# Encoder trunk on one core: in each attention step the 18 gate products stand directly behind the scores

## The chip, the core and the metric

The kernel runs on one core of a Trainium2 chip. A core has TensorE (PE, matrix products and transposes), VectorE (DVE), ScalarE (ACT), GpSimd (POOL) and SyncE (SP), each with its own list of instructions that it works through in the order written; they meet only at semaphores. Products land in PSUM, which has eight banks. The metric is the device time of one execution in microseconds (us); lower is better.

## What is computed

Two layers work on 256 tokens of width 1024. Each layer first mixes tokens in three branches (latent attention with 8 heads, a spatial gating branch, attention to a memory of 256 rows with 4 heads), weighs each branch by a sigmoid gate per channel, and adds the result; then comes a feed-forward part, dense in the first layer and with 8 experts in the second.

```python
def memory_branch(q_raw, mem_n, w_mkv):
    q = q_raw.reshape(b, s, X_HEADS, X_HEAD_DIM) * (X_HEAD_DIM ** -0.5)
    kv = mem_n @ w_mkv
    sc = jnp.einsum('bshd,bmhd->bhsm', q, k).astype(jnp.float32)
    pr = jax.nn.softmax(sc, axis=-1).astype(v.dtype)
    return jnp.einsum('bhsm,bmhd->bshd', pr, v).reshape(b, s, BRANCH_WIDTH)

for l in range(DEPTH):
    h = rmsnorm(x, g_mix[l])
    p = h @ w_in[l]
    c_q, c_kv, k_r, z_sg, q_x, gate_logits = jnp.split(p, SPLITS, axis=-1)
    y_a = mla_branch(c_q, c_kv, k_r, positions, ...)       # 8 heads
    y_b = spatial_gating_branch(z_sg, g_sg[l], w_s[l], b_s[l])
    y_c = memory_branch(q_x, mem_n, w_mkv[l])              # 4 heads
    ys = jnp.stack([y_a, y_b, y_c], axis=2)
    yd = jnp.einsum('bsnw,nwd->bsnd', ys, w_br[l])
    gates = jax.nn.sigmoid(gate_logits.reshape(b, s, N_BRANCH, d) + b_gate[l])
    x = x + jnp.sum(gates * yd, axis=2) @ w_out[l]
    ...
```

## The kernel before

All products are float32 made of three: each operand is split into a high part (`whi`, made by ACT in `hi_parts`) and the rest (`wlo`, made by DVE in `lo_parts`), and high by high, high by rest and rest by high are summed. Weights come in pieces of 1 MB. There are three pairs of `whi`/`wlo` buffers, so a piece can be split when the piece three before it has been used up on PE.

The change is in the attention part of the mixer, which each of the two layers passes once (about 104 to 200 us and 532 to 628 us in the trace). There the heads' work is interleaved with the products of the gates and of the branch outputs. `mixer_steps` writes the order, and PE, ACT and DVE all walk through this one list:

- The memory heads: step i holds `ms` i (scores of head i), `mpT` i-1 (transposes of the softmax of the head before), `mo` i-2 (its product with the values, of the head before that) and one `fill`.
- The transposes `qT` and `kT` of queries and keys.
- The latent heads: step i holds `as` i (scores), `apT` i-1, `O` i-2 and one `fill`.

A `fill` is 18 products of `branch`, which the text below calls the 18 gate products though some are of a branch output. Four fills (parts 0 to 3) make one half of one branch: 48 gate products (tokens t=0 and t=1 in banks 6 and 7), then 24 output products (`br`, 12 for t=0 and 12 for t=1). The gate sum for t=0 ends with part 1, that for t=1 in part 2. The `br` sum for t=1 starts with the seventh product of part 3, and takes a PSUM bank there. The 16 fills stand in the 6 steps of the memory part and the 10 of the latent part. Products 0 to 15 in the texts are fills 0 to 15.

What ACT and DVE do for each entry of the list:

- `ms`/`as`: DVE takes the row maximum from the bank (`rmax`, then `nmax`), ACT the exponential (`pbuf`, line 1558). For memory heads DVE also multiplies by the reciprocal sum (line 2031), and `mpT` waits for that.
- `mpT`/`apT`: ACT copies the transposed softmax out of its bank (line 1566), which frees the bank and is what `mo`/`O` reads. This is called copy i below.
- `mo`: ACT writes `yT_hi` (line 1575), DVE `yT_lo` (line 2042). DVE then also rotates queries (lines 1975 to 1980) behind `mo` 0 and 1, and keys behind `mo` 2.
- `fill` of part 1 or 2: DVE adds the gate bias (`gate_add`, line 1987), then ACT takes the tanh (`gate_tanh`, line 1537). Part 3: DVE multiplies gate and output (`gate_merge`, line 1998).
- Before an entry, ACT and DVE split those weight pieces whose buffer is free by then (`room`).

PSUM banks are given out by `plan_psum`, which walks through the same list: scores, transposes, `mo` and `br` take the low bank that was given out longest ago. So the order of the list sets the banks too. `claim` on PE waits until the bank's last reader has freed it.

Of the kernel before, what the change touches and what calls it, by code (L numbers as in the profile page):

```python
# [60 lines left out]
def plan_psum(depth, heads, x_heads, fcd, nblk):  # L61
# [16 lines left out]
    for l in range(depth):  # L78
# [24 lines left out]
        for step in mixer_steps(heads, x_heads):  # L103
            if step[0] == "fill":
                n, half, part = filled(step[1])
                if part == 0:
                    for t in range(2):
                        take(("gate", l, n, half, t), bank=6 + t)
                elif part > 1:
                    take(("br", l, n, half, part - 2), oldest=low, held=4)  # L110
            elif step[0] in ("as", "apT"):
                take((step[0], l) + step[1:], oldest=low)
            elif step[0] != "O":
                take((step[0], l) + step[1:], oldest=(0, 1, 2, 3, 4, 5))
# [80 lines left out]
def mixer_steps(heads, x_heads):  # L195


    steps = []
    fill = list(range(16))
    for i in range(x_heads + 2):  # L200
        if i < x_heads:
            steps.append(("ms", i))
        if i == 0:
            steps += [("k", 0), ("k", 1), ("v", 0), ("v", 1)]
        if 1 <= i <= x_heads:
            steps.append(("mpT", i - 1))
        if i >= 2:
            steps.append(("mo", i - 2))
        steps.append(("fill", fill.pop(0)))
    for n in range(2):  # L210
        for t in range(2):
            steps += [("qT", t, n), ("kT", t, n)]
    for i in range(heads + 2):
        if i < heads:
            steps.append(("as", i))
        if 1 <= i <= heads:
            steps.append(("apT", i - 1))
        if i >= 2:
            steps.append(("O", i - 2))
        steps.append(("fill", fill.pop(0)))  # L220
    assert not fill
    return steps


def build(nc, x, mem, positions, g_mix, w_in, g_q, g_kv, w_uq, w_uk, w_uv, g_sg, w_s, b_s, g_mem,
# [21 lines left out]
    JOBS = NE * (-(-SEQ // CAP))  # L247
    QS, XS = QK ** -0.5, (BW // XH) ** -0.5
    steps = mixer_steps(H, XH)
    groups = plan_psum(DEPTH, H, XH, FCD, NM)  # L250

# [2109 lines left out]
```

## Time and profile before

| | |
|---|---|
| median of 3 runs | 1666.54 us (1666.48 to 1667.35) |
| the profiled execution's own time | 1666.63 us |
| its span, first to last instruction | 1664.5 us |
| PE busy | 1645.5 us, 99% of the span |
| DVE busy | 1286.9 us, 77% |
| ACT busy | 1057.5 us, 64% |
| longest waits of PE in the attention part | 0.57 and 1.72 us, in each layer |
| granted TensorE clock, mean | 0.998 |

PE is busy nearly all the time. Where it is idle within the attention part, the trace names what it waited for. A row of the timeline gives the start, the duration, engine and line, and in brackets the idle time before it and what ended that. The trace gives an instruction's own duration, but successors on ACT and DVE often start about 0.1 us before it ends; so the distance from start to start is used where two rows follow each other directly.

### The profile page before, as it was taken

Reading aid. Unit: us, or ns where it says so; the run is one execution under the profiler, and the core shown is the slowest. Engines: PE = TensorE matmul, PEld = TensorE weight load, DVE = VectorE, ACT = ScalarE, POOL = GpSimd, SP = SyncE. Lnnn points to the kernel's source line nnn. Section 1 sums busy time; section 2 is a strip of 40 time slices with the busy share of each in tenths; the row PEclk is TensorE's granted clock in tenths of the full one; section 3 lists DMA queues with packets and bytes.
Section 4 is the critical chain, followed back from the end, with each engine's and each line's share of the span. In section 5 each row is a group of like instructions: output and inputs, shape, how many; then the busy total and the mean of one; then the engine's idle time right before and its main releaser. Section 6 shows DMA issues by size and latency. Waiting matters only on the chain.

```text
span 1664.5 us, 22805 instructions
## 1 busy us (share of the span) xinstructions
PE 1645.5 (99%) x8464; PEld 1398.3 (84%) x8464; DVE 1286.9 (77%) x1163; ACT 1057.5 (64%) x961; POOL 30.0 (2%) x57
## 2 busy tenths in 40 slices
PE   9999999999999999999999999999999999999997
PEld 8988889999899788888888888888888888888885
DVE  7576567555566747698888888888888888888997
ACT  6554436433465454477777777777777777777775
POOL 1000000000000000020000000000000000000100
PEclk9999999999999999999999999999999999999999
DMA  7753488885366435699999999999999999999994
GB/s 234 230 169 136 140 279 299 270 263 191 103 198 194 144 128 176 253 357 393 395 394 390 354 395 388 359 391 385 364 380 385 372 394 360 387 380 366 396 393 160
DMA packets 243426, 496.98 MB, mean 299 GB/s; under 512 B 8534, under 2 KB 64400, under 8 KB 243360
## 3 DMA queue, kind: packets, MB, share of 16 engines
q1 hardware_dynamic: 237360, 479.23, 80.2%
q0 software_dynamic: 2624, 8.45, 1.6%
q10 hardware_dynamic: 3376, 8.39, 1.3%
q8 instruction: 44, 0.72, 0.2%
q14 instruction: 22, 0.18, 0.0%
HBM read 476.64 MB, written 19.40 MB: 298 GB/s over the span
## 4 chain that ended last, share of the span: by engine, by line
PE 91%; DVE 4%; ACT 2%; issue 2%; DMA 1%; DVEq 0%; POOL 0%; ACTq 0%
PE bank L1142 25%; PE bank L681 20%; PE bank L1175 19%; PE bank L1146 12%; PE bank L852 9%; PE bank L1159 1%; DVE wlo L1804 1%; PE bank L671 1%; ACT whi L1423 1%; PE bank L966 1%; DMA hn<-in_mem 1%; ACT pbuf L1558 0%; PE bank L938 0%; PE bank L1187 0%; DVE rmax L2023 0%
## 5 line engine op out<-in xcount | busy, mean ns | idle before, releaser
L2218 DVE TENSOR_TENSOR wlo<-raw,whi 128x2048 fp32r<-128x2048 f32 x328 | 748.1, 2289 | 108.0 <-ACT whi L1660 108.0
L1660 ACT ACTIVATE whi<-raw 128x2048 fp32r<-128x2048 f32 x328 | 627.7, 1918 | 177.4 <-PE bank L1146 94.1
L1804 DVE TENSOR_TENSOR wlo<-raw,whi 128x2048 fp32r<-128x2048 f32 (+3 forms) x121 | 259.4, 2148 | 183.5 <-ACT whi L1423 182.2
L1142 PE MATMUL bank<-whi,yT_hi 128*128 128x512 f32 x896 | 352.5, 396 | 0.0
L1142 PE MATMUL bank<-whi,yT_lo 128*128 128x512 f32 x896 | 347.4, 390 | 0.0
L1423 ACT ACTIVATE whi<-raw 128x2048 fp32r<-128x2048 f32 (+3 forms) x121 | 217.7, 1803 | 134.6 <-PE bank L681 100.4
L1146 PE MATMUL bank<-wlo,yT_hi 128*128 128x512 f32 x896 | 240.0, 390 | 0.0
L1146 PEld LDWEIGHTS bank<-wlo,yT_hi 128*128 128x128 f32 x896 | 168.2, 188 | 35.6
L1142 PEld LDWEIGHTS bank<-whi,yT_lo 128*128 128x128 f32 x896 | 168.3, 188 | 33.7 <-DVE yT_lo L2186 0.2
L1142 PEld LDWEIGHTS bank<-whi,yT_hi 128*128 128x128 f32 x896 | 168.3, 188 | 33.5
L1175 PE MATMUL bank<-whi,yT_hi 128*128 128x512 f32 x448 | 176.0, 393 | 0.0
L1175 PE MATMUL bank<-wlo,yT_hi 128*128 128x512 f32 x448 | 174.6, 390 | 0.0
L1175 PE MATMUL bank<-whi,yT_lo 128*128 128x512 f32 x448 | 174.5, 390 | 0.0
L681 PE MATMUL bank<-hT_hi,whi 128*128 128x256 f32 x464 | 131.4, 283 | 0.0
L681 PE MATMUL bank<-hT_hi,wlo 128*128 128x256 f32 x464 | 131.3, 283 | 0.0
L681 PE MATMUL bank<-hT_lo,whi 128*128 128x256 f32 x464 | 131.3, 283 | 0.0
L1175 PEld LDWEIGHTS bank<-whi,yT_hi 128*128 128x128 f32 x448 | 84.0, 188 | 25.2 <-issue 8.7
L1175 PEld LDWEIGHTS bank<-wlo,yT_hi 128*128 128x128 f32 x448 | 84.1, 188 | 17.8
L1175 PEld LDWEIGHTS bank<-whi,yT_lo 128*128 128x128 f32 x448 | 84.1, 188 | 16.2
L681 PEld LDWEIGHTS bank<-hT_lo,whi 128*128 128x128 f32 x464 | 89.0, 192 | 0.4
L681 PEld LDWEIGHTS bank<-hT_hi,whi 128*128 128x128 f32 x464 | 89.0, 192 | 0.4
L681 PEld LDWEIGHTS bank<-hT_hi,wlo 128*128 128x128 f32 x464 | 89.0, 192 | 0.0
(287 smaller groups left out, 2016.7 us busy)
## 6 DMA issues: line engine op xcount, KB each, us to landing
raw<-in_moe_w SPq DMA_DIRECT2D x336, 1024.0 KB, 7.4
raw<-in_w_in SPq DMA_DIRECT2D x36, 1024.0 KB, 5.1
raw<-in_dense_w SPq DMA_DIRECT2D x30, 1024.0 KB, 6.6
raw<-in_w_br SPq DMA_DIRECT2D x12, 1024.0 KB, 5.1
raw<-in_w_out SPq DMA_DIRECT2D x8, 1024.0 KB, 5.1
rows_by_slot<-qxT SPq DMA_DIRECT2D x15, 512.0 KB, 7.1
raw<-in_w_mkv SPq DMA_DIRECT2D x6, 1024.0 KB, 8.4
y_by_slot<-qxT SPq DMA_DIRECT2D x9, 512.0 KB, 7.7
```

What stands on the lines that cost most here:

```text
L671: ins = nc.tensor.matmul(bank, lhs(k), rhs(k), start=(k == 0), stop=(k == n - 1))
L681: ins = nc.tensor.matmul(bank, lhs(a, k), rhs(b, k), start=(start and k == chunks[0] and a + b == 0), stop=(stop and k == chunks[-1] and a ...
L852: ins = nc.tensor.matmul(bank, src(a, x0), w[b_][:, w0, :], start=(start and q + i == 0), stop=(stop and last))
L966: ins = nc.tensor.matmul(b[:, t * SEQ:(t + 1) * SEQ], qT[0:QK, h, tok(t)], kT[0:QK, h, :], start=True, stop=True)
L1142: nc.tensor.matmul(b[:, :], hselT[a][:, half, tok(k)], w[:, k, :], start=(half + k + a == 0), stop=False)
L1146: ins = nc.tensor.matmul(b[:, :], hselT[0][:, half, tok(k)], w[:, k, :], start=False, stop=(half == 1 and k == 3))
L1159: ins = nc.tensor.transpose(b[:, tok(c)], g32_m[:, tok(c)], ident[:, :])
L1175: ins = nc.tensor.matmul(banks[4 + n][:, :], gated_m[a][:, b_ % 2, tok(2 * half + c)], w[p][:, c, n * HALF:(n + 1) * HALF], start=(b_ + ha ...
L1423: nc.scalar.activation(whi[:, m % SPLIT, 0:floats(n)], raw[:, pieces[n][1], 0:floats(n)], ACT.Copy).then_inc(hi_ready, 1)
L1660: nc.scalar.activation(whi[:, (E0 + n) % SPLIT, :], raw[:, n % RAW, :], ACT.Copy).then_inc(hi_ready, 1)
L1804: V.tensor_tensor(wlo[:, m % SPLIT, 0:size], raw[:, pieces[n][1], 0:size], whi[:, m % SPLIT, 0:size].bitcast(F32), ALU.subtract).then_inc( ...
L2218: V.tensor_tensor(wlo[:, s, :], raw[:, n % RAW, :], whi[:, s, :].bitcast(F32), ALU.subtract).then_inc(lo_ready, 1)
```

## The change

In every step of the list that has scores, the fill moves from the end of the step to directly behind the scores. In the steps without scores (the last two of the memory part and of the latent part) it stays at the end. Nothing is added or removed.

```diff
@@ -202,22 +202,28 @@
             steps.append(("ms", i))
         if i == 0:
             steps += [("k", 0), ("k", 1), ("v", 0), ("v", 1)]
+        if i < x_heads:
+            steps.append(("fill", fill.pop(0)))
         if 1 <= i <= x_heads:
             steps.append(("mpT", i - 1))
         if i >= 2:
             steps.append(("mo", i - 2))
-        steps.append(("fill", fill.pop(0)))
+        if i >= x_heads:
+            steps.append(("fill", fill.pop(0)))
...
     for i in range(heads + 2):
         if i < heads:
             steps.append(("as", i))
+        if i < heads:
+            steps.append(("fill", fill.pop(0)))
         if 1 <= i <= heads:
             steps.append(("apT", i - 1))
         if i >= 2:
             steps.append(("O", i - 2))
-        steps.append(("fill", fill.pop(0)))
+        if i >= heads:
+            steps.append(("fill", fill.pop(0)))
```

The changed kernel's lines are 6 higher than those of before (938 becomes 944, and so on).

The first place is ACT at the memory heads, from the exponential of head 1 on (`pbuf,rsum` line 1558; `whi` line 1423 is a split, `cT` line 1537 a tanh, `pbuf<-bank` line 1566 a copy of transposes). Before:

```order
L1558 ACTIVATE pbuf,rsum<-bank2,nmax 128x256 x2
L1566 ACTIVATE pbuf<-bank4 128x512
L1423 ACTIVATE whi<-raw 128x2048
L1537 ACTIVATE cT<-cT 128x512
L1558 ACTIVATE pbuf,rsum<-bank5,nmax 128x256 x2
L1566 ACTIVATE pbuf<-bank3 128x512
L1575 ACTIVATE yT_hi<-bank0 128x256
L1423 ACTIVATE whi<-raw 128x2048
L1537 ACTIVATE cT<-cT 128x512
L1558 ACTIVATE pbuf,rsum<-bank2,nmax 128x256 x2
```

And now, the same engine and place in the changed kernel, ending with the copy and the `yT_hi` behind the exponential of head 3:

```order
L1564 ACTIVATE pbuf,rsum<-bank2,nmax 128x256 x2
L1429 ACTIVATE whi<-raw 128x2048
L1543 ACTIVATE cT<-cT 128x512
L1572 ACTIVATE pbuf<-bank4 128x512
L1564 ACTIVATE pbuf,rsum<-bank5,nmax 128x256 x2
L1429 ACTIVATE whi<-raw 128x2048
L1543 ACTIVATE cT<-cT 128x512
L1572 ACTIVATE pbuf<-bank0 128x512
L1581 ACTIVATE yT_hi<-bank1 128x256
L1564 ACTIVATE pbuf,rsum<-bank2,nmax 128x256 x2
L1429 ACTIVATE whi<-raw 128x2048
L1572 ACTIVATE pbuf<-bank4 128x512
```

The copy of a head's transposes (and `yT_hi`) stood ahead of the split and the tanh; it now stands behind both.

The second place is PE around the products 3 of the memory heads. In the changed kernel, from the transposes of head 1 (`ident,pbuf`) over `mo` 0 and the scores of head 3 to the seventh product of the fill (six products in bank 3 are cut to two rows):

```order
L944 MATMUL bank0<-ident,pbuf 128x128 [waits bank_free0,prob_ready]
...
L677 MATMUL bank1<-pbuf,mv 128x256 [waits bank_free2,bank_free1,bank_free4]
...
L924 MATMUL bank2<-mkT,qxT 128x256 [waits bank_free2]
...
L858 MATMUL bank3<-whi,yT_hi 128x512
L858 MATMUL bank3<-wlo,yT_hi 128x512
...
L858 MATMUL bank0<-whi,yT_hi 128x512 [waits bank_free0]
```

Before, from the same transposes to the same product (behind `mo` 0 stands a whole fill, its last row shown):

```order
L938 MATMUL bank3<-ident,pbuf 128x128 [waits bank_free3,prob_ready]
...
L671 MATMUL bank0<-pbuf,mv 128x256 [waits bank_free2,bank_free0,bank_free1,bank_free4]
...
L852 MATMUL bank1<-whi,yT_lo 128x512
L918 MATMUL bank2<-mkT,qxT 128x256 [waits bank_free2]
...
L938 MATMUL bank4<-ident,pbuf 128x128 [waits bank_free4,prob_ready]
...
L671 MATMUL bank5<-pbuf,mv 128x256 [waits bank_free5,bank_free3]
...
L852 MATMUL bank3<-whi,yT_hi 128x512 [waits bank_free3]
```

The `br` sum for t=1 takes bank 0 in the changed kernel, which the transposes of head 1 used shortly ahead of it, so its first product waits for copy 1. Before, it took bank 3, also used by the transposes of head 1, but a whole fill and the transposes of head 2 stood between them and the fill of part 3, and copy 1 stood early on ACT.

The third place is ACT at the end of the latent heads, from the exponential of head 7 on (`pbuf,asum`). Before, and then now:

```order
L1558 ACTIVATE pbuf,asum<-bank2,nmax 128x256 x2
L1566 ACTIVATE pbuf<-bank3 128x512
L1423 ACTIVATE whi<-raw 128x2048
L1537 ACTIVATE cT<-cT 128x512
L1566 ACTIVATE pbuf<-bank1 128x512
```

```order
L1564 ACTIVATE pbuf,asum<-bank1,nmax 128x256 x2
L1429 ACTIVATE whi<-raw 128x2048
L1543 ACTIVATE cT<-cT 128x512
L1572 ACTIVATE pbuf<-bank2 128x512
L1572 ACTIVATE pbuf<-bank3 128x512
```

Copy 6 went from ahead of the split and the tanh of products 13 to behind them. On PE, `O` 6 stood behind products 13 and `apT` 7; it still does, but `apT` 6 and `O` 5, which were ahead of products 13, are now between them and `apT` 7.

## Rows read from the trace of the kernel before

**Rows 1.** The page's part 1: busy time, share, instructions of each engine.

```profile
PE 1645.5 (99%) x8464; PEld 1398.3 (84%) x8464; DVE 1286.9 (77%) x1163; ACT 1057.5 (64%) x961; POOL 30.0 (2%) x57
```

**Rows 2.** Waits of PE, whole span: total us, times, longest.

```profile
PE bank L938 <- DVE pbuf L2031: 4.6, 4, 1.7
```

**Rows 3.** Timeline of PE, memory heads of layer 0: start, duration, instruction.

```profile
110.78 1.02 PE L918 MATMUL bank<-mkT,qxT 128*128 128x256 f32 x4
111.64 0.62 PE L938 MATMUL bank<-ident,pbuf 128*128 128x128 f32 x4
112.09 1.03 PE L671 MATMUL bank<-pbuf,mv 128*128 128x256 f32 x4
112.77 0.58 PE L852 MATMUL bank<-whi,hT_hi 128*128 128x512 f32 x1
...
117.06 1.02 PE L918 MATMUL bank<-mkT,qxT 128*128 128x256 f32 x4
...
126.01 0.66 PE L938 MATMUL bank<-ident,pbuf 128*128 128x128 f32 x4 [1.72 <-DVE pbuf L2031]
126.50 1.03 PE L671 MATMUL bank<-pbuf,mv 128*128 128x256 f32 x4
127.18 0.58 PE L852 MATMUL bank<-whi,hT_hi 128*128 128x512 f32 x1
```

**Rows 4.** Timeline of ACT, memory heads of layer 0.

```profile
109.67 0.47 ACT L1558 ACTIVATE pbuf<-bank,nmax 128x256 f32<-128x256 f32 x1 [3.73 <-DVE nmax L2025]
...
115.94 0.63 ACT L1537 ACTIVATE cT<-cT 128x512 f32<-128x512 f32 x1 [2.96 <-DVE cT L1987]
116.74 0.47 ACT L1558 ACTIVATE pbuf<-bank,nmax 128x256 f32<-128x256 f32 x1 [0.17 <-DVE nmax L2025]
...
117.65 0.59 ACT L1566 ACTIVATE pbuf<-bank 128x512 f32<-128x512 f32 x1
118.13 0.39 ACT L1575 ACTIVATE yT_hi<-bank 128x256 fp32r<-128x256 f32 x1
118.39 1.93 ACT L1423 ACTIVATE whi<-raw 128x2048 fp32r<-128x2048 f32 x1
```

**Rows 5.** Timeline of DVE, memory heads of layer 0.

```profile
113.01 2.29 DVE L1804 TENSOR_TENSOR wlo<-raw,whi 128x2048 fp32r<-128x2048 f32 x1 [1.47 <-ACT whi L1423]
115.22 0.69 DVE L1987 TENSOR_TENSOR cT<-bank,cqkv 128x512 f32<-128x512 f32 x1
115.82 0.68 DVE L2023 TENSOR_REDUCE rmax<-bank 128x2 f32<-128x512 f32 x1
116.53 0.17 DVE L2025 TENSOR_SCALAR nmax<-rmax 128x2 f32<-128x2 f32 x1
...
117.99 0.62 DVE L2031 TENSOR_SCALAR pbuf<-pbuf,rrec 128x256 f32<-128x256 f32 x2
118.62 0.42 DVE L2042 TENSOR_TENSOR yT_lo<-bank,yT_hi 128x256 fp32r<-128x256 f32 x1
118.96 0.28 DVE L1975 TENSOR_TENSOR sgv<-raw,cos_t 128x128 f32<-128x128 f32 x1
...
120.35 2.29 DVE L1804 TENSOR_TENSOR wlo<-raw,whi 128x2048 fp32r<-128x2048 f32 x1
```

**Rows 6.** Timeline of PE, latent heads of layer 0: scores of heads 3, 7, then O 6.

```profile
157.84 1.03 PE L966 MATMUL bank<-raw 96*128 96x256 f32 x4
...
183.10 1.03 PE L966 MATMUL bank<-raw 96*128 96x256 f32 x4
...
189.85 1.00 PE L671 MATMUL bank<-raw,pbuf 128*128 128x64 f32 x8
```

**Rows 7.** Timeline of PE and of DVE: products 14, and the maximum of head 3.

```profile
190.66 0.48 PE L852 MATMUL bank<-whi,hT_hi 128*128 128x512 f32 x1
...
158.91 0.69 DVE L2023 TENSOR_REDUCE rmax<-bank 128x2 f32<-128x512 f32 x1 [0.18 <-PE bank L966]
```

**Rows 8.** Busy time in windows at the end: window, its length, engines (count), PEclk, DMA, GB/s.

```profile
1656.00:1658.00 2.00, 0.00 (x0) 0.00 (x0) 1.70 (x7) 0.76 (x3) 0.00 (x0) 1.00 0.01 4
1658.00:1660.00 2.00, 0.00 (x0) 0.00 (x0) 1.76 (x10) 0.55 (x1) 0.00 (x0) 0.56 0.04 8
```

## The prediction

> **What bounds the kernel now.** I read the page's busy times first: PE is busy for 1645.5 of 1664.5 us [rows 1]. No more than 19 us of idle PE can be won, and whatever PE loses anywhere is nearly all added to the time, because nothing behind it has slack in which to make it up. Next I read who PE waits for. In the attention part its only sizeable wait is that of the transposes `mpT` for DVE's scaled softmax, 4.6 us in four waits, two in each layer [rows 2]; the last one in layer 0 is 1.72 us ahead of `mpT` 3 [rows 3]. The third view is the timeline of ACT and DVE at that place [rows 4, 5]. It shows why the softmax is late. The memory heads are bound by one ring through two engines. DVE splits a piece (113.01), adds the gate bias (115.22), takes the maximum (115.82 and 116.53), ACT takes the exponential (116.74), copies (117.65, 118.13) and splits the next piece (118.39), and DVE takes that up again at 120.35. That is 7.34 us a round, from split to split. PE's own work in a round is 0.86 us for the scores, 0.45 for the transposes, 0.68 for `mo` and 4.29 for the fill, 6.3 us in all [rows 3]. So here PE waits for the ring, and the question is whether the change makes the ring shorter or longer.
>
> **What the change seems to give.** `mpT` i-1 now has two fills between it and its scores, not one. For `mpT` 1 and 2 the wait of 0.57 us or less goes. For `mpT` 3 it does not, for there the fill of the next step stays at the end: between the scores of head 3 and `mpT` 3 lie one fill, `mpT` 2 and `mo` 1, as before. If that were all, the change would win at most the 4.6 us of [rows 2].
>
> **What it costs, the memory heads.** ACT and DVE follow the same list. Copy i-1 and `yT_hi` i-2 now stand behind the split and the tanh of the fill, and DVE's `yT_lo` and rotation behind split and bias. Before, these ran in the shadow: while ACT split (118.39), DVE did `yT_lo` and the rotation (118.62 to 120.35) [rows 4, 5]. Now they come one after the other. I follow layer 0 from the exponential of head 1, which nothing ahead of it moves (109.67 [rows 4]). Distances from start to start, from [rows 4, 5]: exponential to the next on ACT 0.91, copy to next 0.48, `yT_hi` to next 0.26, ACT split to DVE split 1.96, split to bias 2.21, bias to tanh 0.72, bias to maximum 0.60, maximum to nmax 0.71, nmax to exponential 0.21, exponential to scaling 1.25, scaling to next 0.63, `yT_lo` to rotation 0.34, rotation 1.39. The rows show that an instruction's successor starts 0.1 us before its duration is over; so tanh to next is 0.53 and ACT split to next 1.82.
>
> - Step 1: ACT split 110.58, DVE split 112.54, bias 114.75, tanh 115.47, copy 0 at 116.00. Maximum 115.35, nmax 116.06, exponential 2 behind copy 0 at 116.48.
> - Step 2: ACT split 117.39, DVE split 119.35, bias 121.56, tanh 122.28, copy 1 at 122.81 (ends 123.40), `yT_hi` 0 at 123.29. DVE must wait for that: `yT_lo` at 123.71, rotation 124.05, maximum of head 3 at 125.44, nmax 126.15, exponential 126.36, scaling 127.61, done 128.24.
> - Step 3: behind the exponential ACT splits (127.27) and only then does copy 2, 129.09 to 129.68.
>
> PE in the same time, in its new order: scores 2 at 110.9, fill 2 at 111.8, `mpT` 1 at 116.1, `mo` 0 at 116.6 (copy 0), scores 3 at 117.3, fill 3 at 118.2. Its seventh product comes up at 119.8, but bank 0 is freed by copy 1 at 123.4, so PE stands for **3.6 us**. The fill ends at 126.2, `mpT` 2 and `mo` 1 at 127.3, and `mpT` 3 waits for DVE until 128.3, **0.9 us**. `mo` 2 could go at 128.7, but copy 2 ends at 129.7: another **1.0 us**. Products 4 start at 130.4, where they started at 127.18 [rows 3]. The same work of PE lies ahead of them in both orders, so the memory heads lose **3.2 us**. Products 5, `qT` and `kT` follow in the old order, with their neighbours on DVE and ACT shifted as much.
>
> **The latent heads.** No reciprocal is needed there and the rotation is gone, so the late copies have a full step of cover: by the same distances, copy 2 ends some 3 us and copy 3 some 2 us ahead of the `O` that reads it. The last copy with a tanh ahead of it has no such cover: `O` 6 follows products 13 after 0.45 us of `apT` 6, 0.81 us of `O` 5 and 0.44 us of `apT` 7, where a whole fill lay between before. In the clock of the rows (without the 3.2 us): scores 7 are at 183.10 [rows 6], now about 182.9, since a small wait of 0.2 us ahead of scores 2 goes with the fill. The maximum comes 1.07 us behind the scores (157.84 to 158.91 [rows 6, 7]), at 183.97; exponential 184.89, ACT split 185.80, DVE split 187.76, bias 189.97, tanh 190.69, copy 6 at 191.22, ended 191.81. PE has done products 13 at 188.0 and `apT` 7 at 189.7, and waits **2.1 us** for copy 6. Products 14 start 0.81 us behind `O` 6 (189.85 to 190.66 [rows 6, 7]), at 192.7 and not at 190.66: the latent heads lose **2.0 us**. Split, tanh and both `O` behind that shift alike.
>
> **The sum.** 3.2 + 2.0 = 5.2 us a layer. Layer 1 repeats layer 0 (the four waits of [rows 2] are two equal pairs), so 10.4 us. Against the profiled execution's own 1666.63 us that gives 1677.0, and against the median of 1666.54 us, 1676.9 us. Nothing else is moved: SP and POOL have the same lists, and a piece's load is asked for at the same point of the ring and has a round or two to land. The price of the products is unchanged, 0.24 us each, 4.29 us for 18 [rows 3].
>
> **The clock.** The longest new idle time of PE is 3.6 us. At the end of the kernel PE is idle from about 1654 on; in 1656 to 1658 the granted clock is still 1.00 (2.4 GHz), in 1658 to 1660 it is 0.56, on its way to 1.2 GHz [rows 8]. So the trace bears out an idle time of this length without a fall, though not by much. The Trainium skill ("TensorE: Matmul & The Clock Gate", the section on why this matters for your kernels) warns of idle gaps between bursts of matmuls, since an idle TensorE goes to its lower clock and comes back only after sustained work. By that rule this change would cost more than my sum, the time of the clock's rival below instead of 1676.9 us; the trace's tail agrees that idleness lowers the clock, and no row shows it lowered within the kernel.
>
> **The rivals.**
>
> *Faster: the late copies are hidden.* The mechanism is the one for which the order looks made: two fills cover the softmax, copies arrive in time, and the waits of [rows 2] go. That gives 1666.5 - 4.6 = 1661.9 us. It decides at the seventh product of fill 3: copy 1 would have to end before 119.8, and the chain puts it at 123.4. For it speaks only that the bank wait does not exist in the trace of before and is derived. I give it 7%.
>
> *No change.* The ring is as long as it was (7.34 us a round) if DVE's rotation still runs under ACT's split, and the new waits only take the place of the old ones: 1666.5 us, within 0.2%. Against it speaks that `yT_lo` has to wait for `yT_hi`, which is behind the tanh. 8%.
>
> *Only one of the two places.* If only the memory heads lose, 2 x 3.2 = 6.4 us, 1672.9 us; if only `O` 6, 2 x 2.0, 1670.5 us. 10%.
>
> *The clock falls as well.* If the idle time ahead of the seventh product of fill 3 drops the clock to half, products take 0.48 us instead of 0.24. A whole fill of them costs 4.3 us more, in each layer; nothing to 8.6 us on top of 10.4, 1677 to 1685.5 us. 8%.
>
> *The change does not do what it says.* The order of all engines shows that it does; I give this nothing.
>
> **How the numbers follow.** The forecast has 67%, and its own range is 1673 to 1681 us: the chain has some twenty links, each good to a few hundredths, and two layers. The predicted time is 1676.9 us. The range for 8 in 10 goes from 1671 us (one place alone) to 1682 us (a part of the clock's price). Faster by over 0.2% (3.3 us, about what a measurement of this kernel can tell from no change) has 0.07, within it 0.08, slower 0.85.
>
> **What would show it.** PE's waits: an idle time of about 3.6 us inside the fill (line 858) ended by ACT's copy (line 1572), one of about 0.9 us at the transposes (944) ended by DVE, one of 1.0 and one of 2.1 us at the value products (677) ended by ACT's copy, each twice; the wait of 0.57 us gone. On ACT, copy 1 at about 122.8 us, behind a tanh. The start of the products 4 at 130.4 and not 127.2 us. I am wrong if the seventh product of fill 3 does not wait, if copy 6 ends before `apT` 7, or if PE's clock is below 1.00 in the attention part.

## The result and the profile after

The changed kernel takes 1682.95 us (median of 4 runs, 1680.03 to 1683.32) against 1666.55 us before. The ratio is 1.0095, with a 95% interval of 1.0082 to 1.0107: slower by 16.4 us. The direction was forecast, and so were the places; the size was not. The forecast was 1676.9 us, and the range ended at 1682 us, 0.95 us short. The profiled execution took 1683.32 us, its span is 1681.3 us, so the two traces differ by 16.8 us.

PE's busy time went up as well, from 1645.5 us [rows 1] to 1653.0 us, although it does the same 8464 products. That is the first sign that something else than waiting was added. Part 1 of the page after:

```profile
PE 1653.0 (98%) x8464; PEld 1403.2 (83%) x8464; DVE 1286.8 (77%) x1163; ACT 1057.5 (63%) x961; POOL 29.4 (2%) x57
```

DVE and ACT are unchanged. The waits of PE over the whole span (total us, times, longest), where [rows 2] had 4.6 us in four waits at line 938:

```profile
PE bank L858 <- ACT pbuf L1572: 6.8, 2, 3.4
PE bank L677 <- ACT pbuf L1572: 6.0, 6, 2.1
```

The waits for DVE's softmax are gone, as intended. In their place PE waits for ACT's copies of the transposes: twice 3.4 us inside a fill (line 858) and six times at the value products (line 677). That makes 12.8 us against 4.6 us, 8.2 us more; the other 8.6 us must be somewhere else. Most of them are the 7.5 us by which PE's busy time grew. The list of waits also has 1.5 us for DVE's split at the start of the kernel (10 to 23 us), but scores 2 of the memory heads start at 110.88 us where they started at 110.78, so the part ahead of the change costs no more than 0.1 us.

The timeline of PE in the memory heads of layer 0 shows both kinds of loss. It answers to [rows 3]:

```profile
119.46 0.39 PE L858 MATMUL bank<-wlo,yT_hi 128*128 128x512 f32 x1
119.69 0.40 PE L858 MATMUL bank<-whi,yT_lo 128*128 128x512 f32 x1
123.50 0.50 PE L858 MATMUL bank<-whi,yT_hi 128*128 128x512 f32 x1 [3.41 <-ACT pbuf L1572]
...
125.16 0.63 PE L858 MATMUL bank<-whi,yT_hi 128*128 128x512 f32 x1
125.58 0.63 PE L858 MATMUL bank<-wlo,yT_hi 128*128 128x512 f32 x1
...
127.72 0.84 PE L944 MATMUL bank<-ident,pbuf 128*128 128x128 f32 x4
...
130.47 1.13 PE L677 MATMUL bank<-pbuf,mv 128*128 128x256 f32 x4 [0.61 <-ACT pbuf L1572]
131.25 0.58 PE L858 MATMUL bank<-whi,hT_hi 128*128 128x512 f32 x1
```

Ahead of the stall the products start 0.23 us apart. The seventh waits until 123.50. From 125.16 on, they start 0.42 to 0.43 us apart (125.16, 125.58): the array runs at about half its rate. The products 4 start at 131.25 us and not at 127.18.

The windows say what the granted clock was (window, its length, busy us of the engines with counts, PEclk, DMA share, GB/s):

```profile
120.00:124.00 4.00, 0.59 (x3) 0.46 (x3) 2.48 (x3) 1.39 (x3) 0.54 (x1) 1.00 0.27 55
124.00:128.00 4.00, 4.00 (x13) 3.07 (x13) 2.81 (x12) 1.02 (x4) 0.00 (x0) 0.60 0.70 272
196.00:200.00 4.00, 3.97 (x14) 3.45 (x15) 0.00 (x0) 0.46 (x1) 0.00 (x0) 0.57 0.98 323
560.00:564.00 4.00, 4.00 (x11) 3.13 (x10) 2.81 (x12) 1.02 (x4) 0.00 (x0) 0.50 0.67 262
```

The window with the stall still has the full clock (the third value from the end). In the one behind it the mean is 0.60, so most of it ran at the lower level, 1.2 GHz and not 2.4. In layer 1 (560 to 564) the whole window is at the lower level: the twelve products behind the stall start 0.43 us apart, or more. The window from 196 lies behind the wait for copy 6.

ACT's timeline shows why the stall is there. It answers to [rows 4]:

```profile
117.45 1.92 ACT L1429 ACTIVATE whi<-raw 128x2048 fp32r<-128x2048 f32 x1
122.33 0.63 ACT L1543 ACTIVATE cT<-cT 128x512 f32<-128x512 f32 x1 [2.96 <-DVE cT L1993]
122.87 0.58 ACT L1572 ACTIVATE pbuf<-bank 128x512 f32<-128x512 f32 x1
123.34 0.38 ACT L1581 ACTIVATE yT_hi<-bank 128x256 fp32r<-128x256 f32 x1
126.42 0.47 ACT L1564 ACTIVATE pbuf<-bank,nmax 128x256 f32<-128x256 f32 x1 [2.70 <-DVE nmax L2031]
```

Copy 1 (122.87) stands behind the tanh (122.33), which stands behind DVE's split and bias; ACT itself is idle for 2.96 us meanwhile. DVE in turn, in the rows that answer to [rows 5]:

```profile
121.61 0.68 DVE L1993 TENSOR_TENSOR cT<-bank,cqkv 128x512 f32<-128x512 f32 x1
123.82 0.42 DVE L2048 TENSOR_TENSOR yT_lo<-bank,yT_hi 128x256 fp32r<-128x256 f32 x1 [1.52 <-ACT yT_hi L1581]
...
125.50 0.68 DVE L2029 TENSOR_REDUCE rmax<-bank 128x2 f32<-128x512 f32 x1
...
127.67 0.61 DVE L2037 TENSOR_SCALAR pbuf<-pbuf,rrec 128x256 f32<-128x256 f32 x2
```

DVE waits 1.52 us for `yT_hi`, then rotates, and only then takes the maximum of head 3, at 125.50. The two engines wait for each other in turn, where before they worked side by side.

At the end of the latent heads, PE ahead of and behind `O` 6 (answering to [rows 6, 7]):

```profile
193.33 0.61 PE L944 MATMUL bank<-ident,pbuf 128*128 128x128 f32 x4
196.03 1.59 PE L677 MATMUL bank<-raw,pbuf 128*128 128x64 f32 x8 [2.09 <-ACT pbuf L1572]
197.38 0.77 PE L858 MATMUL bank<-whi,hT_hi 128*128 128x512 f32 x1
197.96 0.63 PE L858 MATMUL bank<-wlo,hT_hi 128*128 128x512 f32 x1
```

`O` 6 waits 2.09 us for copy 6, needs 1.35 us from its start to the next row where it needed 0.81, and products 14 start slowly.

### The profile page after: what moved, and what is told of

It is laid out like the page before. It is cut to its first block, busy times and chain, and to the rows that moved or that the text cites. A ratio compares the mean times of both kernels' runs of the same rounds, so it can differ in the third digit from the quotient of the medians.

```text
span 1681.3 us, 22819 instructions
## 1 busy us (share of the span) xinstructions
PE 1653.0 (98%) x8464; PEld 1403.2 (83%) x8464; DVE 1286.8 (77%) x1163; ACT 1057.5 (63%) x961; POOL 29.4 (2%) x57
## 4 chain that ended last, share of the span: by engine, by line
PE 90%; DVE 4%; ACT 3%; issue 2%; DMA 1%; SPq 0%; DVEq 0%; ACTq 0%
PE bank L1148 24%; PE bank L687 20%; PE bank L1181 18%; PE bank L1152 12%; PE bank L858 9%; ACT whi L1429 2%; PE bank L1165 1%; DVE wlo L1810 1%; PE bank L677 1%; PE bank L972 1%; DMA x_sb<-in_x 1%; ACT pbuf L1564 0%; SPq L1303 0%; DVE cT L1993 0%; PE bank L1193 0%
```

## The experiments

The theory after the result has two parts. First, the chain: fills with a tanh or a split now stand ahead of the copies on ACT, which makes PE wait as worked out. Second, the clock: the waits lower it, and the work behind them is slow for a few microseconds. The rivals are that the chain costs more than worked out and the clock nothing, that the bank given out by the planner is the cause, and that PE's order itself costs the time. Another cause of the low clock is possible too: in the three windows above with a lowered clock the DMA engines are busy (0.67 to 0.98).

**The two places apart.** One kernel changes the memory heads alone:

```diff
     for i in range(heads + 2):
         if i < heads:
             steps.append(("as", i))
-        if i < heads:
-            steps.append(("fill", fill.pop(0)))
         ...
-        if i >= heads:
-            steps.append(("fill", fill.pop(0)))
+        steps.append(("fill", fill.pop(0)))
```

> The change in the memory heads alone; the latent heads have the order of before. Theory (ring through ACT and DVE, and the clock falls behind the long wait): the trace of the changed kernel has its products 4 late by 4.0 us in layer 0 and 5.0 us in layer 1, so 1666.5 + 9.0 = 1675.5 us, granted clock below 1.00 behind the wait of 3.4 us. Rival (the chain alone, clock without effect): 1666.5 + 6.4 = 1672.9 us, all products 0.23 us apart.

Measured: 1675.13 us, ratio 1.0049 (1.0032 to 1.0066), 8.3 us over the 1666.81 us of before in these runs; expected were 9.0. The other kernel does the same edit in the memory part, so that only the latent heads are changed:

> The change in the latent heads alone. Theory (copy 6 late, then the clock falls): 3.8 us a layer as in the trace of the changed kernel, 1674.1 us, with a wait of 2.1 us ahead of O 6 and slow products 14. Rival (chain alone): 2.0 us a layer, 1670.5 us. Together with the kernel that changes the memory heads alone the two costs should add to the 16.4 us of the whole change if the places are independent.

Measured: 1674.0 us, ratio 1.0048 (1.0031 to 1.0066), 7.2 us over before; expected were 7.6. Together they cost 15.5 us against 16.4 us of the whole change, which fits two independent places. It is a weak check, for the four runs of the second kernel lie at 1671.13, 1671.89, 1676.11 and 1677.33 us, so its median falls between two pairs and its closeness to the forecast of 1674.1 us is partly luck. I had not expected this spread. The mean granted clocks of these runs are 0.998, 0.997, 0.995 and 0.994 in the same order: the longer the run, the lower its clock. Only the second was profiled, and its trace shows how a clock can fall or not. In both layers `O` 6 waits equally long (the rows of layer 0, then of layer 1):

```profile
191.65 1.39 PE L674 MATMUL bank<-raw,pbuf 128*128 128x64 f32 x8 [2.09 <-ACT pbuf L1569]
...
623.48 1.10 PE L674 MATMUL bank<-raw,pbuf 128*128 128x64 f32 x8 [2.09 <-ACT pbuf L1569]
```

and the windows behind the two waits show a lowered clock in layer 0 and none in layer 1:

```profile
192.00:196.00 4.00, 4.00 (x15) 3.38 (x15) 0.00 (x0) 0.08 (x1) 0.00 (x0) 0.57 0.98 324
624.00:628.00 4.00, 4.00 (x22) 3.37 (x21) 0.00 (x0) 0.50 (x1) 0.00 (x0) 1.00 0.94 314
```

In the same 4 us, 15 instructions of PE fell into the one and 22 into the other (among them a few narrow products of `O` 6). So the same wait of 2.09 us costs the clock in one place and not in another of one execution, with the DMA engines as busy in both (0.98 and 0.94). Where in the longest run its further 5.4 us arose, no trace shows. The wait of 1.72 us of the kernel before [rows 3] never did in its trace.

**The clock by itself.** The changed kernel, with products on the identity matrix in the waits, into banks that are free then and that the next real product starts anew:

```diff
                         for t in range(T):
+                            if (n, half, t) == (1, 0, 1):
+                                keep_clock(("gate", l, 1, 1, 0), 14)
                             b = claim(("br", l, n, half, t))
...
                     else:
+                        if h == H - 2:
+                            keep_clock(("br", l, 2, 1, 0), 8)
                         read(pe, ("apT", l, h))
```

> The changed kernel with products on the identity matrix, whose results nobody reads, in the two waits of each layer: 14 ahead of the seventh product of fill 3, 8 ahead of O 6. Theory (idle time lowers the clock, the rest of the cost is the chain): the clock stays at 1.00, the waits on ACT's copies are the same in sum but filled, and the time is the chain's own, 1666.5 + 10.4 = 1676.9 us. Rival (the products are slow for another reason, or the chain costs more than worked out): no change from 1683 us.

Measured: 1677.76 us (1677.57 to 1677.87), ratio 1.0066 (1.0049 to 1.0083). PE's timeline shows the 14 extra products (each is two instructions there, hence x28) and the same end of the wait:

```profile
119.87 3.29 PE L711 MATMUL bank<-ident 128*128 128x128 f32 x28
...
123.44 0.50 PE L858 MATMUL bank<-whi,yT_hi 128*128 128x512 f32 x1 [0.29 <-ACT pbuf L1576]
...
128.29 0.66 PE L946 MATMUL bank<-ident,pbuf 128*128 128x128 f32 x4 [0.52 <-DVE pbuf L2041]
...
130.50 0.58 PE L858 MATMUL bank<-whi,hT_hi 128*128 128x512 f32 x1
```

Copy 1 still comes at the same time (PE goes on at 123.44 and not 123.50), but the products behind it keep their 0.23 us and the products 4 start at 130.50, where the prediction had 130.4. The window behind the second wait has its full clock, with the DMA engines busy (0.95) as they were in the changed kernel:

```profile
196.00:200.00 4.00, 4.00 (x21) 3.37 (x21) 0.00 (x0) 0.61 (x1) 0.00 (x0) 1.00 0.95 323
```

Work that computes nothing makes the kernel 5.2 us faster (1682.95 to 1677.76). That is what the lowered clock costs in the changed kernel; the remaining 11.2 us are the chain (11.0 us against the 1666.81 us of before in these runs). DMA traffic alone is not the cause of the fall, for it is the same here and the clock stays. The two traces, 5.7 us apart, also show where the clock's price arose. Against the kernel with the clock held up, the changed kernel falls back by 0.7 us in the memory heads and 1.6 us in the latent heads of layer 0, and by 1.8 and 1.6 us in layer 1. The memory heads of layer 0 lose less, because slow products there run partly in time that PE would have waited for the softmax anyway.

**The order on ACT and DVE.** PE keeps the changed order and its banks, ACT and DVE walk through the list of before, which `late=True` makes (the loop on ACT is shown; the one on DVE is edited alike):

```diff
+    late_steps = mixer_steps(H, XH, late=True)
...
-                for step in steps:
+                for step in late_steps:
```

> PE in the changed order with its banks, ACT and DVE in the order of before (copies and the rotation ahead of split and tanh). Theory (the ring's order on ACT and DVE costs the time): copy 1 at about 118, no bank wait, copy 6 ahead of O 6; only mpT 3 waits, until about 126.5 us and so 2.7 us; products 4 within 0.5 us of before, 1667.5 us, and up to 4 us more if the clock falls in that wait. Rival (PE's own order and its banks cost the time): 1675 us or more.

Measured: 1672.41 us (1671.56 to 1673.15), ratio 1.0034 (1.0022 to 1.0047): 10.5 us less than the changed kernel, with PE's order the same. The 3.4 us inside the fill and the wait at `O` 6 are gone, so the order on the other two engines did cost them. The rival is not wholly wrong, though: with PE's order alone the kernel is still 5.6 us above before, and 0.9 us above the end of what was expected. Two rows of PE show the rest:

```profile
126.39 0.66 PE L945 MATMUL bank<-ident,pbuf 128*128 128x128 f32 x4 [2.48 <-DVE pbuf L2038]
127.83 1.71 PE L678 MATMUL bank<-pbuf,mv 128*128 128x256 f32 x4 [0.78 <-ACT pbuf L1573]
```

`mpT` 3 waits 2.48 us as foreseen. The 0.78 us at `mo` 2 were not: since a fill now stands ahead of the transposes on PE, `room` finds a buffer free one entry earlier and puts the split ahead of the copy on ACT, even in the old list (split at 125.38 us, copy 2 at 127.18; before, copy 2 at 124.99 and the split at 125.73). And the clock fell behind these waits (`mo` 2 takes 1.71 us, where it took 1.03; the granted clock of 128 to 132 us is 0.57). Products 4 start at 128.97 us, 1.8 us late.

**The bank.** The changed kernel, with bank 4 for the `br` sum of fill 3:

```diff
                 elif part > 1:
-                    take(("br", l, n, half, part - 2), oldest=low, held=4)
+                    take(("br", l, n, half, part - 2), held=4,
+                         oldest=(4,) if (n, half, part) == (1, 0, 3) else low)
```

> The changed kernel, but the br sum for t=1 of fill 3 takes bank 4 (last used by the transposes of head 0), so that nothing in that fill waits for copy 1. Theory (the softmax of head 3 is late through the order on ACT and DVE; the bank only decides where PE stands): the 3.4 us inside the fill go, mo 1 waits 0.4 us for copy 1 and mpT 3 waits some 4 us until 128.3, products 4 start no earlier than 130.4 us, and since the slow stretch now falls on them and not ahead of a wait the time is 1683 to 1686 us. Rival (the bank given out by the planner is the cause): 6.8 us less than the changed kernel, 1676 us.

Measured: 1684.41 us (1683.42 to 1684.89), ratio 1.0104 (1.0089 to 1.0119), as the theory has it. The wait inside the fill is gone, and nothing is won:

```profile
123.60 1.10 PE L678 MATMUL bank<-pbuf,mv 128*128 128x256 f32 x4 [0.34 <-ACT pbuf L1573]
128.36 1.11 PE L945 MATMUL bank<-ident,pbuf 128*128 128x128 f32 x4 [3.65 <-DVE pbuf L2038]
...
131.31 0.99 PE L859 MATMUL bank<-whi,hT_hi 128*128 128x512 f32 x1
132.09 0.63 PE L859 MATMUL bank<-wlo,hT_hi 128*128 128x512 f32 x1
```

PE now stands 3.65 us ahead of `mpT` 3, until the same 128.3 us, and products 4 start at 131.31. The longest wait in a list of waits is where PE happened to stand, not what made it late. Both waits end in the same chain.

This kernel also waits 2.10 us ahead of `O` 6, and here the clock fell later. In layer 1 the wait ends at 634.67 us and `O` 6 itself runs at the full clock:

```profile
632.00:636.00 4.00, 1.90 (x16) 1.62 (x15) 1.47 (x2) 1.60 (x3) 1.06 (x2) 1.00 0.51 118
636.00:640.00 4.00, 4.00 (x12) 3.10 (x11) 0.00 (x0) 0.00 (x0) 0.00 (x0) 0.57 0.79 275
```

**A late chain with more cover.** Memory heads with the fill first also in step 4, bank 4 as above, latent heads as before (the diff shows the memory part against the changed kernel):

```diff
-        if i < x_heads:
+        if i <= x_heads:
             steps.append(("fill", fill.pop(0)))
         ...
-        if i >= x_heads:
+        if i > x_heads:
             steps.append(("fill", fill.pop(0)))
```

> Memory heads with the fill first in steps 0 to 4 (the changed kernel leaves it last in step 4) and bank 4 for the br sum; latent heads as before. Theory: the ring is as late as in the changed kernel (softmax 3 at 128.3 us), but two fills stand between scores 3 and mpT 3, so PE waits only 0.3 us (mo 0), 0.4 us (mo 1) and 0.8 us (mo 2), no clock loss, products 5 at 131.3 us against 132.2 before: 1665 us. Rival (the late ring costs in any order): 1673 us or more.

Measured: 1666.71 us (1666.31 to 1669.33), ratio 1.0002 (0.9992 to 1.0011). PE no longer waits for the late softmax with two fills ahead of `mpT` 3, but the gain that I had worked out did not come either; the estimate missed by 1.7 us. PE's timeline names what was late next:

```profile
129.82 1.99 PE L675 MATMUL bank<-pbuf,mv 128*128 128x256 f32 x8 [0.55 <-ACT pbuf L1570]
...
139.69 1.19 PE L961 MATMUL bank<-ident,raw 128*96 128x128 f32 x8 [1.16 <-DVE raw L2065]
```

The second row is the transposes of queries and keys. They wait 1.16 us for DVE to empty a bank, where they waited 0.23 us before. DVE worked without a pause from the softmax on and reached these copies at 138.95 us, 0.2 us later than before (138.76); PE was there 0.7 us earlier.

**Only the fills that put nothing into the ring.** From the kernel before, the fill goes ahead in steps 3 and 4 alone:

```diff
     for i in range(x_heads + 2):
         ...
+        if i in (x_heads - 1, x_heads):
+            steps.append(("fill", fill.pop(0)))
         if 1 <= i <= x_heads:
             steps.append(("mpT", i - 1))
         if i >= 2:
             steps.append(("mo", i - 2))
-        steps.append(("fill", fill.pop(0)))
+        if i not in (x_heads - 1, x_heads):
+            steps.append(("fill", fill.pop(0)))
```

> The kernel before, with the fill ahead of transposes and value products in steps 3 and 4 of the memory heads alone, everything else in the old order. ACT and DVE do nothing new between the exponential of head 2 and that of head 3, since fills 3 and 4 have no bias and no tanh. Theory (a fill may move ahead where it puts nothing into the ring): both waits at mpT 2 and 3 are covered, products 5 start at 129.9 and not at 132.2 us, 2.3 us a layer, 1662.2 us. Rival (any fill directly behind scores costs): 1667 us or more.

Measured: 1662.37 us (9 runs, 1662.22 to 1662.46), ratio 0.9974 (0.9964 to 0.9983), the fastest of all. No wait for a softmax and none for a copy is left in the memory heads:

```profile
122.07 0.60 PE L941 MATMUL bank<-ident,pbuf 128*128 128x128 f32 x4
122.50 1.03 PE L674 MATMUL bank<-pbuf,mv 128*128 128x256 f32 x4
127.53 0.60 PE L941 MATMUL bank<-ident,pbuf 128*128 128x128 f32 x4
127.96 1.98 PE L674 MATMUL bank<-pbuf,mv 128*128 128x256 f32 x8
...
137.30 1.19 PE L960 MATMUL bank<-ident,raw 128*96 128x128 f32 x8 [0.61 <-DVE raw L2064]
```

Only 0.61 us at the transposes of queries and keys remain. The rule behind it is the one that the changed kernel broke: a fill of part 3 or 0 has no bias and no tanh and asks only two multiplications of DVE, so it may go ahead of the transposes; a fill of part 1 or 2 asks for a split, a bias and a tanh, and these then delay the copies. A split alone still moves here, as ACT shows:

```profile
124.99 1.91 ACT L1426 ACTIVATE whi<-raw 128x2048 fp32r<-128x2048 f32 x1
126.80 0.59 ACT L1569 ACTIVATE pbuf<-bank 128x512 f32<-128x512 f32 x1
```

It puts copy 2 at 126.80 us, where it stood at 124.99, but that ends ahead of `mo` 2 (127.96), since fill 4 covers it. So the fill need not be free of all work for ACT; what it puts ahead of the copies has to fit under the cover.

## Why the prediction was wrong, point by point

- **What bounds the kernel, and the ring through ACT and DVE.** Right. The whole chain that was worked out from the rows of before came out within about 0.1 us: maximum of head 3 predicted at 125.44 and found at 125.50, `yT_lo` at 123.71 and found at 123.82, copy 1 at 122.81 and found at 122.87.
- **The memory heads, 3.2 us a layer.** Right for the chain: with the clock held up, products 4 start at 130.50 (130.4 predicted), 3.3 us late. The stall inside the fill was 3.41 us (3.6 predicted), with the clock held up the one at `mpT` 3 was 0.52 us (0.9) and the one at `mo` 2 0.78 us (1.0); 0.28 us at `mo` 0 had not been counted. In the changed kernel itself the wait at `mpT` 3 does not show, because the slow products fill it.
- **The latent heads, 2.0 us a layer.** The mechanism was right, and the wait (2.09 us for 2.1 predicted) too. The term was a little too small: with the clock held up a layer loses 5.6 us in all (5.5 in layer 1), so 2.3 us here (2.2 in layer 1). The 0.2 us that I counted as won ahead of scores 2 were hardly there: without the 3.3 us, scores 7 would start at 183.1, as before, and not at 182.9.
- **The clock: this is the step that failed.** The sum put this term at nothing. I read the tail of the kernel ([rows 8]) as evidence that PE can be idle for 3.6 us at full clock, gave the fall 8%, and cut the range at 1682 us. The tail shows one idle stretch, and I had no row at all on shorter waits such as the one ahead of `O` 6. The runs show that the clock fell behind both waits in both layers of the changed kernel, behind 3.41 and 3.42 us and behind 2.09 us twice, and in another kernel behind one of two equal waits. It cost 5.2 us where the sum had none, and the four runs of the changed kernel differ by 3.3 us. The price that the rival named, nothing to 8.6 us on top of 10.4, held it, but partly by luck: it was worked out for the fill alone, and 3.2 of the 5.7 us between the two traces arose behind `O` 6, which the rival did not name. By the Trainium skill ("TensorE: Matmul & The Clock Gate", the section on why this matters for your kernels), idle gaps between bursts of matmuls bring the lower clock back. The traces agree behind the 3.41 and 3.42 us, and show it behind 2.09 us as well, though not each time; I should have given the rule more weight than the single row against it. Of my own signs of being wrong, the one on the clock came true.
- **The sum.** 10.4 us were predicted for the chain, and 11.2 us were found (1677.76 against 1666.55). The other 5.2 us are the clock.
- **The rivals.** "Faster" was wrong at the place that it named: the seventh product of fill 3 did wait. "No change" failed since `yT_lo` did wait for `yT_hi`, 1.52 us. "One place alone" is excluded by the two kernels that change one place each, at 8.3 and 7.2 us. The wait ahead of `mpT` 2 went, as I had it, and is worth less than what came in its place.

Left open: whether a fall of the clock behind a wait of about 2 us follows anything that a program can control. Behind 2.09 or 2.10 us the traces show a fall twice in the changed kernel, twice with the other bank and once in two in the kernel of the latent heads; behind the 2.48 and 2.50 us of the kernel with the old order on ACT and DVE they show it both times.

## What to carry to other kernels

Moving cover work on one engine moves, in a list that all engines share, the work that this cover asks of the other engines: ask for each fill what it puts ahead of the copies that the next products read, and move only those whose work there still ends in time. In a chain through two engines, follow their rows link by link from one fixed point; distances from start to start gave times good to 0.1 us here. Where a new idle time of TensorE comes out of such a chain, add the slow products behind it to the sum as a likely term and not as an afterthought.

## What the runs showed of the hardware

- The granted clock fell behind idle times of PE of 3.4 us, 2.5 us and 2.09 us, to the lower of its two levels (1.2 GHz and not 2.4), and then products started 0.43 us apart instead of 0.23 us, for some 3 to 6 us. The idle times of 1.72 us and less in the kernel before were followed by none. The same wait of 2.09 us in one execution was followed by a mean of 0.57 in one layer and of 1.00 in the other. Where it fell, the fall came at different distances: some 1.5 us behind the end of the 2.10 us wait with the other bank, and ahead of the end of the 3.41 us stall in the kernel of the memory heads (mean 0.83 in 120 to 124 us; the first product behind the stall, at 123.31, is slow already).
- Products without use in a wait, 14 and 8 of them a layer, kept the clock up and made the kernel 5.2 us faster; they cost no visible time themselves, since each wait ended within 0.1 us of where it ended without them or earlier.
- The kernels in which such waits stand spread more from run to run: 1671.1 to 1677.3 us for the latent heads alone, with mean granted clocks from 0.998 down to 0.994, against 0.3 us between the runs with the clock held up.
